# Modulation vectors of the keys, the values and the second layer: row sums on VectorE and a closing sum over partitions, in place of vector-matrix products on TensorE

## The reference, cut to what matters

```python
c_act = silu(c)                                    # (1, 1024)
for layer in range(2):
    mod = c_act @ mod_w[layer] + mod_b[layer]      # 1024 x 6144
    sh1, sc1, g1, sh2, sc2, g2 = split(mod, 6)
    u = rms_norm(h, norm_mix[layer]) * (1 + sc1) + sh1
    mix = hgrn2_mixer(u, ...) if layer == 0 else chunk_band_attention(u, k_pad, v_pad, ...)
    h = h + g1 * mix
    u = rms_norm(h, norm_ffn[layer]) * (1 + sc2) + sh2
    h = h + g2 * swiglu(u, ffn_w_in[layer], ffn_w_out[layer])
    if layer == 0:
        shift, scale = split(c_act @ kv_mod_w + kv_mod_b, 2)     # 1024 x 2048
        k_pad, v_pad = split((rms_norm(h, kv_norm) * (1 + scale) + shift) @ kv_w, 2)
```

## Time and profile before

| | |
|---|---|
| runs, median (lowest to highest) | 1661.57 us (1660.62 to 1666.17) |
| profiled execution, device time | 1663.13 us |
| its span, first to last instruction | 1660.7 us |
| mean granted TensorE clock | 0.962 of full |
| busy: TensorE, VectorE, ScalarE | 95%, 39%, 35% |
| DMA over the span | 404.25 MB, mean 243 GB/s |

### The profile page before, as it was taken

How to read it: one execution, slowest core, us unless ns; L and a number is a source line. 1 busy time by engine, 2 the same in 40 slices (tenths; PEclk the granted TensorE clock), 3 DMA queues, 4 the chain that set the end, 5 groups by cost and what they waited for, 6 DMA issues and landing times.

```text
span 1660.7 us, 27926 instructions
## 1 busy us (share of the span) xinstructions
PE 1577.5 (95%) x12058; PEld 1286.9 (77%) x12058; DVE 648.0 (39%) x1105; ACT 582.7 (35%) x928; POOL 28.0 (2%) x47
## 2 busy tenths in 40 slices
PE   6899989999999988999999999999899999999997
PEld 4898879999998964999999869988665655656563
DVE  3657745334445534555545354563311111111110
ACT  2432234333334444544444555543111121211111
POOL 1000000000000100100000000001000000000000
PEclk8799979999998989999998979999999999999999
DMA  9568714888976630455553323543699999999992
GB/s 330 180 205 276 230 53 158 286 286 286 304 254 207 226 102 1 156 194 180 188 184 106 131 76 102 207 148 105 259 421 421 420 421 425 421 421 420 423 423 102
DMA packets 204313, 404.25 MB, mean 243 GB/s; under 512 B 5013, under 2 KB 172210, under 8 KB 196018
## 3 DMA queue, kind: packets, MB, share of 16 engines
q1 hardware_dynamic: 202176, 397.43, 65.6%
q0 software_dynamic: 1648, 5.18, 1.1%
q10 hardware_dynamic: 386, 0.11, 0.0%
HBM read 401.63 MB, written 1.07 MB: 242 GB/s over the span
## 4 chain that ended last, share of the span: by engine, by line
PE 91%; DVE 4%; ACT 3%; issue 1%; DMA 1%; SPq 0%; ACTq 0%; DVEq 0%
PE ps L1709 28%; PE ps L2206 13%; PE ps L1932 7%; PE ps L2228 7%; PE ps L1744 5%; PE ps L2193 4%; PE ps L2238 4%; PE ps L1722 3%; PE ps L1771 3%; PE ps L1755 2%; PE ps L1961 2%; PE ps L1866 2%; PE ps L1791 2%; PE ps L1801 1%; PE ps L1972 1%
## 5 line engine op out<-in xcount | busy, mean ns | idle before, releaser
L1709 PE MATMUL ps<-u,wsplit 128*128 128x256 f32 x3960 | 489.3, 285 | 7.8 <-issue 3.8
L1709 PEld LDWEIGHTS ps<-u,wsplit 128*128 128x128 f32 x3960 | 481.2, 193 | 9.7 <-issue 4.8
L1107 DVE TENSOR_TENSOR wsplit<-arena,wsplit 128x1024 fp32r<-128x1024 f32 x258 | 313.0, 1223 | 356.3 <-ACT wsplit L720 353.6
L720 ACT ACTIVATE wsplit<-arena 128x1024 fp32r<-128x1024 f32 x258 | 268.9, 1055 | 263.4 <-PE ps L1709 114.6
L2206 PE MATMUL ps<-arena 128*64 128x256 f32 x1408 | 155.7, 379 | 0.8 <-DVE arena L1630 0.8
L1635 DVE TENSOR_TENSOR arena<-arena,ps 128x256 f32<-128x256 f32 x32 | 13.5, 421 | 358.7 <-ACT arena L1073 358.7
L2206 PEld LDWEIGHTS ps<-arena 128*64 128x64 f32 x1408 | 101.0, 137 | 60.7 <-issue 12.0
L1932 PE MATMUL ps<-hid,wsplit 128*128 128x256 f32 x1056 | 130.2, 283 | 0.0
L1932 PEld LDWEIGHTS ps<-hid,wsplit 128*128 128x128 f32 x1056 | 128.2, 192 | 0.0
L1079 ACT ACTIVATE arena<-ps 64x512 f32<-64x512 f32 x64 | 37.9, 592 | 154.0 <-PE ps L2228 153.2
L1744 PE MATMUL ps<-wsplit,u 128*128 128x256 f32 x672 | 85.5, 289 | 0.0
(11 more groups left out here) (331 smaller groups left out, 1386.9 us busy)
## 6 DMA issues: line engine op xcount, KB each, us to landing
arena<-in_w SPq DMA_DIRECT2D x66, 2048.0 KB, 16.8
late<-in_w SPq DMA_DIRECT2D x30, 2048.0 KB, 17.1
arena<-in_mod_w SPq DMA_DIRECT2D x48, 1024.0 KB, 7.5
arena<-in_ffn_w_in SPq DMA_DIRECT2D x44, 1024.0 KB, 5.2
arena<-in_ffn_w_out SPq DMA_DIRECT2D x22, 1024.0 KB, 6.0
arena<-in_a_w_in SPq DMA_DIRECT2D x16, 1024.0 KB, 8.2
arena<-in_kv_mod_w SPq DMA_DIRECT2D x8, 1024.0 KB, 6.6
arena<-in_kv_w SPq DMA_DIRECT2D x8, 1024.0 KB, 7.8
```

The source lines that it names most:

```text
L720: act.activation(piece_buf(p, 0), piece_src(p), ACT.Copy).then_inc(hi_done, 1)
L1107: dve.tensor_tensor(piece_buf(p, 1), piece_src(p), piece_buf(p, 0).bitcast(F32), ALU.subtract).then_inc(lo_done, 1)
L1709: mm = pe.matmul(o, w_[:, k, :], u[:, x_, k, :], start=first, stop=last)
```

## The change

The 32 gemv slots become 32 "rows" slots. Such a slot holds 128 whole rows (one chunk k of the 1024) of 2048 neighbouring columns, 8 KB in a piece. Four stretches of 8 slots cover the same 8192 columns: one for keys and values, three for the second layer. VectorE (`weighted_rows`) multiplies slot k by the activated `c` of its partitions and adds it to a running total of 128 x 2048, one instruction per slot. When a stretch is complete, TensorE (`columns`) adds the total over the partitions: 16 products by a column of ones. The two totals that alternate lie in parts of the arena that are idle then.

24 rows slots stand in the feed-forward of the first layer (3 in iterations 0 and 1, then 2, none in the last), 8 among the keys and values, one after each lin slot. `columns` stands at the end of iterations 3, 7 and 11 and behind the transposes of the memory. The gains of the second feed-forward (`last_gains`) are now made behind the queries.

```diff
+    def rows_slot():
+        n, k = divmod(len(stretch_slots), DC)
+        s = slot("rows", "modkv" if n == 0 else "mod1", 2048 * max(n - 1, 0))
...
             if with_gemv:
-                jobs[f"gemv_ffn{i}"] = []
-                for _ in range(3 if i < 8 else 2):
...
+                if i < FFI:
+                    jobs[f"rows_ffn{i}"] = [rows_slot() for _ in range(3 if i < 2 else 2)]
...
+    for i in range(8):
+        linear("kv_k" if i < 4 else "kv_v", "kv", 256 * i, 1, "act")
+        jobs["rows_kv"].append(rows_slot())
...
                     if old["kind"] == "gemv":
                         sp.wait_ge(gemv_mm, gemv_of[old["n"]] + 1)
+                    elif old["kind"] == "rows":
+                        sp.wait_ge(rows_done, old["row_count"])
...
+            def weighted_rows(s):
+                stretch, k, total = s["stretch"], s["k"], rows_sum[s["stretch"] % 2]
+                dve.wait_ge(slot_in[s["n"] % RING], slot_use(s["n"]))
+                if k == 0:
+                    if stretch >= 2:
+                        dve.wait_ge(gemv_col, stretch + 1)
+                    dve.tensor_scalar(total, slot_dst(s), cact[:, k, 0:1], None, ALU.mult).then_inc(rows_done, 1)
+                else:
+                    dve.wait_ge(rows_done, s["row_count"] - 1)
+                    dve.scalar_tensor_tensor(out=total, in0=slot_dst(s), scalar=cact[:, k, 0:1], in1=total,
+                                             op0=ALU.mult, op1=ALU.add).then_inc(rows_done, 1)
...
                     between(i)
+                    if layer == 0:
+                        weighted_rows(jobs[f"rows_ffn{i}"][0])
                     dve.wait_ge(f_hi, fi + 1)
                     dve.tensor_tensor(hid[:, fi % 2, 1, :, :], hidden[:, i % 2, :, :],
                                       hid[:, fi % 2, 0, :, :].bitcast(F32), ALU.subtract).then_inc(f_lo, 1)
+                    for s in jobs[f"rows_ffn{i}"][1:] if layer == 0 else ():
+                        weighted_rows(s)
...
-            lo_upto(LAST["kv_k"])
+            for n, p in enumerate(jobs["kv_k"]):
+                lo_upto(p["w"])
+                if n % 2 == 1:
+                    weighted_rows(jobs["rows_kv"][n // 2])
...
+            def columns(stretch):
+                pe.wait_ge(rows_done, DC * (stretch + 1))
+                if stretch in (0, 3):
+                    pe.wait_ge(mod_done, {0: 3, 3: 5}[stretch])
+                for m in range(16):
+                    mm = pe.matmul(modps[:, 48 + 16 * stretch + m:49 + 16 * stretch + m],
+                                   rows_sum[stretch % 2][:, P * m:P * (m + 1)], ones[:, 0:1], start=True, stop=True)
+                mm.then_inc(gemv_col, 1)
...
-                    if layer == 0:
-                        gemv(jobs[f"gemv_ffn{i}"])
+                    if layer == 0 and i in (3, 7, FFI):
+                        columns((3, 7, FFI).index(i))
-            column(NG - 1)
...
+            columns(3)
             linears(jobs["b_q"], (u_lo, 24))
```

More of the change, by code:

```diff
@@ L121, in linear @@
                 piece(s, half, job, engine)
-    done = [0]
+    stretch_slots = []
+    def rows_slot():
+        n, k = divmod(len(stretch_slots), DC)
+        s = slot("rows", "modkv" if n == 0 else "mod1", 2048 * max(n - 1, 0))
+        s["stretch"], s["k"], s["row_count"] = n, k, len(stretch_slots) + 1
+        stretch_slots.append(s)
+        return s
     def ffn(layer, with_gemv):
@@ L276, in two_blocks @@
         key_sq = late[:, RING * SLOT:].rearrange("p (c t) -> p c t", c=DC)
+        rows_sum = (part(8192, 2048), part(13312, 2048))
         mem_tok, memT = part(15872, TB, D), part(17920, DC, T)
@@ L326, in slot_src @@
             w = matrices[s["matrix"]]
+            if s["kind"] == "rows":
+                return w[P * s["k"]:P * (s["k"] + 1), s["at"]:s["at"] + 2048]
             if s["kind"] == "out":
@@ L331, in slot_dst @@
         def slot_dst(s):
+            if s["kind"] == "rows":
+                return ring[(s["n"] - len(slots)) % RING]
             return ring[(s["n"] - len(slots)) % RING].rearrange("p (k n) -> p k n", k=2 if s["kind"] == "out" else DC)
@@ L1405, in new_gains @@
             def new_gains():
-                dve.wait_ge(gemv_col, 3)
-                dve.tensor_tensor(mod[:, 48:112], modps[:, 48:112], vec1[:, 48:112], ALU.add).then_inc(mod_done, 1)
+                dve.wait_ge(gemv_col, 5)
+                dve.tensor_tensor(mod[:, 48:96], modps[:, 48:96], vec1[:, 48:96], ALU.add).then_inc(mod_done, 1)
                 dve.wait_ge(mod_done, 5)
                 for g, at, gain_of in ((2, 56, vec2[:, VEC["kv_norm"]:VEC["kv_norm"] + DC]),
-                                       (3, 72, vec2[:, VEC["norm_mix"] + DC:VEC["norm_mix"] + 2 * DC]),
-                                       (4, 96, vec2[:, VEC["norm_ffn"] + DC:VEC["norm_ffn"] + 2 * DC])):
+                                       (3, 72, vec2[:, VEC["norm_mix"] + DC:VEC["norm_mix"] + 2 * DC])):
                     dve.scalar_tensor_tensor(out=gain[:, g, :], in0=mod[:, at:at + DC], scalar=1.0, in1=gain_of,
@@ L1421, in new_gains, with last_gains @@
                 dve.tensor_tensor(weigh[:, :, 1], final, final, ALU.mult).then_inc(mod_done, 1)
+                dve.wait_ge(mod_done, 10)
+            def last_gains():
+                dve.wait_ge(gemv_col, 6)
+                dve.tensor_tensor(mod[:, 96:112], modps[:, 96:112], vec1[:, 96:112], ALU.add).then_inc(mod_done, 1)
                 dve.wait_ge(mod_done, 11)
+                dve.scalar_tensor_tensor(out=gain[:, 4, :], in0=mod[:, 96:96 + DC], scalar=1.0,
+                                         in1=vec2[:, VEC["norm_ffn"] + DC:VEC["norm_ffn"] + 2 * DC],
+                                         op0=ALU.add, op1=ALU.mult).then_inc(mod_done, 1)
             new_gains()
@@ L1432, in _ @@
             dve.tensor_copy(relT[0:HB, 0:NREL], ps[0:HB, 2, 0:NREL]).then_inc(b_relt, 1)
+            for n, p in enumerate(jobs["kv_v"]):
+                lo_upto(p["w"] + 1)
+                if n % 2 == 1:
+                    weighted_rows(jobs["rows_kv"][4 + n // 2])
             lo_upto(LAST["kv_v"] + LOOKAHEAD)
@@ L1438, in _ @@
             lo_upto(LAST["b_q"] + LOOKAHEAD)
+            last_gains()
             attention_dve("B", None)
@@ L2049, in _ @@
             ffn_pe(1, "ffn1")
-            pe.wait_ge(mod_done, 11)
+            pe.wait_ge(mod_done, 12)
             sums("mix_2", [0, 1, 2])
```

19 lines of the change are left out of this document (5 added, 14 removed).

## The result

The changed kernel takes 1641.1 us in the median of three comparable runs (1636.64 to 1644.92), against 1661.6 before. The ratio is 0.9865 (95% interval 0.9832 to 0.9897), so it is faster, by 1.35%. The forecast was 1631, in a range of 1620 to 1644; its own, narrower range was 1624 to 1639. One more run took 4674 us at a mean granted clock of 0.32 and is left out as disturbed (with it the median is 1643.0).

What follows compares the result with a forecast made beforehand. TensorE was taken to bound the kernel, busy 1577.5 of 1660.7 us. Terms 44.7 - 7.2 - 5.3 - 2.2 + 2.3 - 2.0 = 30.3 us less gave 1632.8 profiled, 1631 as median; range 1620 to 1644, own range 1624 to 1639.

Steps and rivals of the forecast that it cites:

- What goes: First feed-forward: removed gemv groups save TensorE 3.96 us, seven times 4.54, and three times 3.00, together 44.7 us.
- The batches: End of iterations 3 and 7: two `columns` batches between dense pieces cost TensorE 3.6 us each, 7.2 us.
- The stalls in iteration 2: After three-sum iterations, gate 2 lands late and VectorE's row sums delay up 2: 0.4 plus 4.9, 5.3 us.
- Nothing late in iterations 3 to 10: Steady iterations 2 to 10: low part 3 us early, gate's load 2 us early, so no stall.
- The clock: First two `columns` batches: granted clock drops, 1.1 us each, 2.2 us; each can cost 0 to 5.1.
- The tail: From the last feed-forward piece to the keys: 14.8 us instead of 17.1, a gain of 2.3 (0.9 to 7).
- Keys and values: Keys to queries: row sums and loads hidden; only the fourth `columns` and clock cost, 2.0 us (1.2 to 6.3).
- VectorE's 4.8 us per pair: Keys and values: two low parts of 1.22 and a 2.33 row sum, hidden behind TensorE's 5.85 us per pair.
- when alone: Steady feed-forward iterations: one 1 MB load takes 5.2 us from issue to landing when no other load runs.
- a rival in which the ring is late in every iteration: Iterations 2 to 10: late gate loads cost 1.5 us each, 13.5 more, time 1645; chance 13%.

Runs made afterwards that it cites:

- short sums: The changed kernel with row-sum multiply-adds on 128 of 2048 columns, loads and order unchanged: 1631.36 us, ratio 0.9832.
- spread sums: The changed kernel with three rows slots in iterations 4 and 8 instead of 0 and 1, first two column batches one iteration later: 1629.68 us, ratio 0.9795.
- second profile: The changed kernel measured and profiled once more without any edit: 1640.0 us, ratio 0.9863.
- late bias: The changed kernel with GpSimd's two attention-bias DMAs held back until the values are nearly done: 1632.25 us, ratio 0.9806.
- both edits: The changed kernel with the bias DMAs held back, three rows slots in iterations 4 and 8, and column batches moved along: 1625.69 us, ratio 0.9775.
- half batches: The kernel with both edits, its first two column batches split into 8 products each at the end of iterations 4, 5, 8 and 9: 1623.69 us, ratio 0.9781.

## Why the prediction came out as it did

**Right, step by step.** From gate 0 to the end of the last down piece it was 237.05 us (269.03 to 506.08) and is 207.23 (269.24 to 476.47), 29.8 less. The terms for this part add up to 44.7 - 7.2 - 5.3 - 2.2 = 30.0.
- What goes: an iteration with three gemv slots became 4.71 us shorter (forecast 4.54), one with two 3.16 (forecast 3.00).
- The batches: 3.49 each (forecast 3.6).
- The stalls in iteration 2: 1.56 + 4.43 = 5.99 us (forecast 0.4 + 4.9 = 5.3). Both were named by place and by mechanism, and short sums and spread sums showed the mechanism. The load's part was larger than forecast (1.56 for 0.4): the load of gate 2 was issued 7.9 us after the start of gate 1 (forecast 7.7) and first used at 16.7, where it was to land at 15.6. VectorE's part was a little smaller.
- Nothing late in iterations 3 to 10: the 2 us to spare for the gate's load were enough.
- The clock: forecast 1.1 for each batch. Measured 1.55 after the first and nothing after the second, and 1.5 more where it fell behind the stall before up 2. Together 3.0 for 2.2.

**The tail: sized wrong, small.** From 476.47 to the keys at 494.47 it takes 18.0 us, forecast 14.8, before 17.1. The gain of 2.3 became a loss of 0.9. Measured by windows (columns as above):

```profile
476.50:478.70 2.20, 2.20 (x23) 2.20 (x21) 1.56 (x4) 2.19 (x4) 0.00 (x0) 0.99 1.10 417
478.70:495.70 17.00, 17.00 (x69) 15.38 (x69) 6.11 (x19) 3.71 (x10) 0.00 (x0) 0.50 0.25 88
```

The low clock lasts 17.0 us. In the kernel before it lasted 10.2 at this place (512.6 to 522.8). It was to begin somewhere in the one-column products, and it begins inside the batch and reaches into the first products of the keys. In the other changed kernels the same tail took 15.1 to 18.0 us, so the length of the fall differs from one execution to the next, and the gain lies between 2.1 and -0.9. The second profile of the same kernel had 15.1, near the forecast. (The row on the clock that the prediction reads as 24 products holds 24 records, which are 12 products.)

**Keys and values: the step that failed.** It read "Two slots per 5.85 us are 358 GB/s, between the 332 and the 421 above, with six slots loaded ahead", and so called the pair hidden. It counted the ring's traffic alone, and it took six slots ahead for as much lead as before. But the rows slots halve the lead of the weights, from six pairs of pieces to three, so that the last load of `kv_w` was no longer landed when GpSimd's two DMAs began. Both rates that the sentence compares with were of stretches without such DMAs. It also took VectorE's 4.8 us per pair for hidden; once the load is late not all of it is, as the row sum between the two low parts adds some 2.0 us to the stall. And the 5.2 us that the prediction calls the time of a load "when alone" is the median of 44 loads of the feed-forward's weights; no row shows a load alone. The term was 2.0 and measured 10.6: the stall 4.99, the low clock on the last pair of values and a little besides 3.2, keys 0.6, and from the end of the values to the queries 1.8. With the late bias the same stretch measured 1.9, so the rest of that term was right, and its error of 8.6 us in this profile (4.6 in the second one) goes with the stream that was left out.

The Trainium skill (DMA: Bandwidth & Descriptors, Queues, rings and completion order) says that each DMA engine takes packets in turn from every queue that has work. The trace agrees: the 1 MB load issued 2.3 us before the bias was not ahead of it. It was first used 19.8 us after its issue, while the bias took from 517.86 to 538.82.

**The sum.** 30.0 and 2.3 and -2.0 were forecast, and 29.8, -0.9 and -10.6 measured. The gate started 0.2 us later, and 3.3 us were gained later in the kernel. That makes 21.4, and the span fell by 21.5 (1660.7 to 1639.2). The direction held. The time lies inside the wide range, near its upper end, but outside the 1624 to 1639 that the forecast gave itself, and that it lies inside the wide one is luck in part. The upper end came of a rival in which the ring is late in every iteration. That rival did not occur; a stall elsewhere, which I had not seen, took its room. And the 3.2 us that the tail lost were given back by 3.3 us after the queries that nobody had forecast.

**Open.** Why the batch at 415.30 is followed by no drop and the one at 341.14 is, with the same products and the same pieces behind both. In the kernel with both edits both were followed by one. Why the second block began 3.3 us shorter, with the same products, is open too. So is which part of the stall in the values a longer lead of the ring would have saved.

## What to carry to other kernels

Before a load stream is called hidden, list every queue that is busy in that stretch, those of other engines too. When a second kind of load enters a ring, the first kind runs fewer useful slots ahead: here the last load of the weights had been issued 29 us before its use and now 14.5 us before it was wanted. When a wait appears behind a slow load, take away each stream in turn. If the removal of either cures it, the sum is the cause, and moving the one that nobody waits for is free: here one line on GpSimd gave 7.8 us. Do not put other work between two parts that a third engine needs together: it costs nothing until the first part is late. Work that comes in uneven portions (three sums, then two) cost 6 us of stalls in the first iterations and nothing in iterations 4 and 8.

## What the runs showed of the hardware

- Dense one-column products let the clock fall with TensorE busy throughout. The changed kernel, before and after the fall:

```profile
340.00:345.00 5.00, 5.00 (x46) 5.00 (x46) 4.29 (x3) 1.06 (x1) 0.00 (x0) 1.00 0.93 308
345.00:349.00 4.00, 4.00 (x23) 4.00 (x23) 0.00 (x0) 0.00 (x0) 0.00 (x0) 0.57 1.09 361
```

  There is no idle time in either window, yet the clock goes to its lower level (1.2 GHz of 2.4) about a microsecond after the dense products have begun again at 344.63 (0.57 over the second window is its lower level from about 345.6 on). The Trainium skill (TensorE: Matmul & The Clock Gate, Why this matters for your kernels) advises against idle gaps between bursts. This fall had none before it. The profiles of seven kernels have whole batches of 32 records (3.63 us) inside the feed-forward. The first batch came with a fall each time (with short sums the fall began inside it), the second in three. Four half batches of 16 records (1.84 us), in one profile, were followed by none.
- A 1 MB load on the ring took 18 to 20 us from issue to first use in four profiles, while 3 MB in short runs were under way on GpSimd's queue and further ring loads behind it, at 353 GB/s in sum (first profile). Without the 3 MB it was there when wanted, 14.5 us after its issue; in the kernel before, such loads landed after 5.7 to 10.9.
- A multiply-add of 128x2048 in fp32, in place, takes 2342 to 2352 ns over all 28, the same whether DMA was busy or not.
